# Twelve projection slots by chunk, the bias table by matmuls beside the gathers, sinks and GLA products on GpSimd

## The reference

```python
mod = silu(c) @ w_ada + b_ada                  # 6144 numbers: shift1, scale1, gate1, shift2, scale2, gate2
h = rms_norm(x, norm1_g) * (1 + scale1) + shift1
proj = h @ w_in                                # q_g k_g v_g a_lr r_g (gated linear attention), q_s k_s v_s
log_a = log_sigmoid(a_lr @ w_gla_alpha + b_gla_alpha) / 16
o_gla = rms_norm(gla(q_g, k_g, v_g, log_a)) * silu(r_g)      # chunks of 64 tokens, 4 heads
o_swa = rms_norm(softmax attention, 8 heads, window of 128, ALiBi, one sink per head)
x = x + gate1 * (concat(o_gla, o_swa) @ w_out)
x = x + gate2 * peer(modulate(x, norm2_g, shift2, scale2))   # top 16 of 128x128 experts, 8 heads
```

## Time and profile before

| what | value |
|---|---|
| times of three runs | 1479.94 us median, 1479.8 to 1480.45 |
| profiled execution | span 1480.7 us, first to last instruction |
| busy in the span | TensorE 1311.9, VectorE 933.9, ScalarE 655.4, GpSimd 390.6 us |
| granted TensorE clock, mean | 0.979 |
| DMA | 422.51 MB, 285 GB/s in the mean; software queue 303.71 MB |

### The profile page before, as it was taken

One profiled execution on the slowest core, in us unless ns is written; L12 is line 12 of the kernel. 1 busy time (PEld: TensorE's weight loads), 2 busy tenths in 40 slices (PEclk: granted clock), 3 DMA queues, 4 the chain that ended last, 5 costly groups with the idle time before them and its releaser, 6 DMA issues.

```text
span 1480.7 us, 21207 instructions
## 1 busy us (share of the span) xinstructions
PE 1311.9 (89%) x6932; PEld 936.0 (63%) x6932; DVE 933.9 (63%) x2248; ACT 655.4 (44%) x1801; POOL 390.6 (26%) x432
## 2 busy tenths in 40 slices
PE   6999979888988777878777887999999998999998
PEld 3889934444443222333222476999998987899897
DVE  6678586766667667667754555655556635655555
ACT  3434434344343333333333335545455248544554
POOL 4111144444544444444444142200001005100000
PEclk9999999999999999999999998999999999999999
DMA  8875599999999999999999621665556630445554
GB/s 332 333 254 200 182 422 420 421 421 421 421 421 422 421 422 421 422 421 422 421 422 421 268 89 37 234 219 182 182 182 238 196 102 14 157 149 188 187 185 144
DMA packets 81341, 422.51 MB, mean 285 GB/s; under 512 B 10144, under 2 KB 11472, under 8 KB 48368
## 3 DMA queue, kind: packets, MB, share of 16 engines
q0 software_dynamic: 46656, 303.71, 50.1%
q1 hardware_dynamic: 33280, 114.68, 23.3%
q10 hardware_dynamic: 1328, 3.15, 0.6%
HBM read 418.88 MB, written 2.62 MB: 285 GB/s over the span
## 4 chain that ended last, share of the span: by engine, by line
PE 55%; DMA 27%; DVE 8%; ACT 5%; issue 2%; POOL 1%; DVEq 0%; ACTq 0%; SPq 0%; POOLq 0%
DMA big<-in_experts,R 26%; PE pacc L1136 8%; PE pu L663 6%; PE pu L664 6%; PE pu L665 6%; PE pu L632 3%; DVE big L2380 3%; PE pu L644 2%; PE pacc L663 2%; PE pacc L664 2%; PE pacc L665 2%; PE pacc L720 2%; PE pacc L722 2%; PE pacc L721 2%; ACT L1455 1%
## 5 line engine op out<-in xcount | busy, mean ns | idle before, releaser
L1136 PE MATMUL pacc<-big,early_l 128*128 128x512 f32 x1024 | 492.7, 622 | 119.5 <-ACT early_l L1455 119.2
L1136 PEld LDWEIGHTS pacc<-big,early_l 128*128 128x128 f32 x1024 | 188.1, 195 | 408.4 <-issue 406.1
L2380 DVE CUSTOM_DVE_ANT_0 big<-big,early_h 128x1024 f32<-128x1024 f32 x256 | 311.8, 1224 | 204.9 <-DMA big<-in_experts,R 203.8
L535 POOL DMA_INDIRECT big<-in_experts,R x256 | 288.1, 1125 | 378.7 <-PE pacc L1136 334.3
L436 DVE TENSOR_TENSOR ring_lo<-ring,ring_hi 128x512 fp32r<-128x512 f32 x328 | 214.7, 696 | 195.0 <-ACT ring_hi L429 194.9
L429 ACT ACTIVATE ring_hi<-ring 128x512 fp32r<-128x512 f32 x328 | 187.6, 620 | 123.5 <-PE pu L665 49.4
L1455 ACT ACTIVATE R<-R 128x1 f32<-128x1 f32 x256 | 51.6, 202 | 322.3 <-DVE R L2380 322.1
L663 PE MATMUL pu<-X2h,ring_hi 128*128 128x256 f32 x512 | 146.2, 286 | 3.2 <-DVE big L2497 3.2
L665 PE MATMUL pu<-X2h,ring_lo 128*128 128x256 f32 x512 | 145.6, 284 | 0.0
L664 PE MATMUL pu<-X2l,ring_hi 128*128 128x256 f32 x512 | 145.4, 284 | 0.0
L663 PEld LDWEIGHTS pu<-X2h,ring_hi 128*128 128x128 f32 x512 | 98.9, 193 | 4.2 <-DVE big L2497 3.6
(11 more groups left out here) (408 smaller groups left out, 2097.4 us busy)
## 6 DMA issues: line engine op xcount, KB each, us to landing
ring<-in_weights SPq DMA_DIRECT2D x216, 512.0 KB, 3.5
big<-in_ada POOLq DMA_DIRECT2D x40, 512.0 KB, 6.3
big<-in_w POOLq DMA_DIRECT2D x12, 512.0 KB, 7.1
big<-in_experts,R POOLq DMA_INDIRECT x256, 20.0
bias_row<-big ACTq DMA_DIRECT2D x1, 1536.0 KB, 19.8
XT<-in_xT ACTq DMA_DIRECT2D x1, 1024.0 KB, 8.2
scr<-in_ada POOLq DMA_DIRECT2D x2, 512.0 KB, 12.3
tk<-in_ada POOLq DMA_DIRECT2D x2, 512.0 KB, 14.0
```

Of the source, the lines that this page charges most:

```text
L535: pool.indirect_dma_start(out=pair_rows[:, m % PAIR_SLOTS, :], out_offset=None, in_=experts_d, in_offset=bass.IndirectOffsetOnAxis(ap=expe ...
L1136: last = mm(paccf[:, tt * D + half * 512:tt * D + (half + 1) * 512], diagonal[:, m % 16, :], pair_rows[:, m % PAIR_SLOTS, D + half * 512:D ...
L2380: v.tensor_tensor_reduce(out=pair_rows[:, m % PAIR_SLOTS, 0:D], in0=pair_rows[:, m % PAIR_SLOTS, 0:D], in1=h2_rows[:, u % TT, :], scale=1. ...
```

## The change

Twelve of the 18 slots of w_in (q_s, k_s, q_g, half of k_g, v_s and three quarters of v_g) are loaded by rows instead of by columns: one array of [8, 128, 1536], 768 KB for each chunk, into four buffers, issued by SyncE when the second half of x has landed. TensorE multiplies chunk c as soon as ScalarE has made it: eight tiles into the eight places of `pacc`, the tokens' four into the two banks of `pu`. Six slots stay in the ring. The first 16 modulation rows come as eight pairs of 1 MB through four buffers. 24 bf16 matmuls on zeros stand at the start.

```diff
+FIRST_TILES, FIRST_TOKENS = 8, 4
+SWA_AFTER = (range(0, 2), range(0), range(2, 6), range(6, 11), range(11, 20))
+BIAS_AT, BIAS_GROUP = 104, 64
@@ SyncE
+            sp.wait_ge(s["x_late_loaded"], 16)
+            for c in range(FIRST_BUFS):
+                first_load(c)
...
+            for c in range(FIRST_BUFS, C):
+                first_load(c)
             for k in range(RING):
-                if k < 2:
-                    sp.wait_ge(s["ada_used"], 8 + 4 * k)
+                if k < RING - 1:
+                    sp.wait_ge(s["first_used"], C + 1 - FIRST_BUFS + k)
+                else:
+                    sp.wait_ge(s["early_psum"], TT + FIRST_TILES)
@@ TensorE
             pe.wait_ge(s["casts_made"], 1)
+            full_array(24, pu[:, 0, 0:T])
+            for c in range(C):
+                if c % 4 == 0:
+                    pe.wait_ge(s["x_sq"], c // 4 + 1)
...
-            for h in range(NH):
-                if h >= 2:
-                    pe.wait_ge(s["row_copied"], h - 1)
-                mm(row_bank(h)[:, 0:BROW], relb_all[0:NB, h, :], oneh[0:NB, :], start=True, stop=True)\
-                    .then_inc(s["row_psum"], 1)
...
             for c in range(C):
                 pe.wait_ge(s["h_chunks"], c + 1)
+                last = mm(pn[0:16, 0:T], walr[:, c, :], HTf[:, c, :], start=(c == 0), stop=(c == C - 1))
...
+                for tt in range(TT):
+                    last = mm(pu[:, tt, :], HTf[:, c, tt * P:(tt + 1) * P], w[:, FIRST_TILES * P:FIRST], start=(c == 0),
+                              stop=(c == C - 1))
...
+                for j in range(FIRST_TILES):
+                    last = mm(pacc[:, j, :], w[:, j * P:(j + 1) * P], HTf[:, c, :], start=(c == 0 and j % 2 == 0),
+                              stop=(c == C - 1), skip_group_check=True)
+                    if c == C - 1:
+                        last.then_inc(s["early_psum"], 1)
+                        if j == 2:
+                            log_decay()
...
-            for i in range(17):
+            for i in range(5):
+                if i < 2:
+                    pe.wait_ge(s["tok_out"], i + 1)
...
                 if i == 0:
+                    pe.wait_ge(s["consts_made"], 2)
+                    pe.wait_ge(s["la_parts"], 1)
+                    pe.wait_ge(s["tok_out"], TT)
+                    pe.wait_ge(s["early_out"], FIRST_TILES)
+                for step in SWA_AFTER[i]:
+                    if step == 18:
+                        pe.wait_ge(s["gla_ops"], 1)
+                        pe.wait_ge(s["att_biased"], swa_units)
+                        gla_scores(0)
+                    swa_step(step)
+            gla_scores(1).then_inc(s["gla_scores"], 1)
```

A load of a chunk from the fifth on waits until TensorE has used the buffer (`first_used`). On ScalarE the twelve outputs are copied out as two of 128x512 and eight of 128x256: two before the log decay's Identity, Abs, Exp and Ln, six behind them, then the slots 0 and 1 of the ring, then the five exponents, then slot 2 and the softmax units. On GpSimd:

```diff
+            pool.wait_ge(s["ex_done"], 1)
+            pool.wait_ge(s["early_out"], FIRST_TILES)
+            pool.wait_ge(s["evacs"], USE["w_in"] + 1)
+            for u in range(4, SPAN["swa"][1]):
+                sink(u)
+                if u < 4 + 3 + NSUB:
+                    gla_product(u - 4)
+                if u % 2:
+                    row_load(2 * C + 12 + (u - 5) // 2)
```

A sink waits for the exponent of the unit four before it, and VectorE's maximum waits for the sink. VectorE's share loses the sink copies and the products and shifts the modulation:

```diff
-            modulation(2 * C, 6)
+            modulation(2 * C, 8)
...
-                if i < 12:
-                    modulation(2 * C + 6 + i, 1)
-                if 8 <= i < 8 + 3 + NSUB:
-                    gla_product(i - 8)
+                if 2 <= i < 14 and i % 2 == 0:
+                    modulation(2 * C + 8 + (i - 2) // 2, 1)
...
-            modulation(2 * C + 18, 4)
+            modulation(2 * C + 14, 4)
...
-            modulation(2 * C + 22, 2)
+            modulation(2 * C + 18, 2)
...
-            late_modulation(MOD_EARLY)
-            late_modulation(MOD_EARLY + 1)
+            modulation(2 * C + 20, 2)
...
             split_low(dve, v, "w_out", 2)
+            modulation(2 * C + 22, 1)
             out_residual(1)
             split_low(dve, v, "w_out", 3)
+            modulation(2 * C + 23, 1)
```

Three late rows then stand behind the residuals 5, 6 and 7 of the first token tile, the fourth behind the last residual. The bias table is built beside the gathers 104 to 231, two tokens each, from the one-hot rows (64 partitions: the table's rounded part and its remainder):

```diff
+                for t in bias_tokens(m):
...
+                    last = mm(pu[:, group % 2, t % BIAS_GROUP * NH:(t % BIAS_GROUP + 1) * NH], oneh_r[0:2 * NB, T - 1 - t:T - 1 - t + P],
+                              relb_r[0:2 * NB, :], start=True, stop=True)
```

369 lines of the change are left out of this document (198 added, 171 removed).

## The result

Median 1503.77 us after, 1479.96 before; the ratio is 1.0162, with a 95% interval of 1.0147 to 1.0176. That is slower, as forecast, but by 23.8 us in place of 8.5, and 6.8 above the upper end of the range. One of the changed kernel's four runs took 1555.71 us at a mean granted clock of 0.83 in place of 0.97; it counts in no ratio, and the median without it is 1503.66. The spans of the two profiled executions differ by 21.0 us (1501.7 against 1480.7). The other 2.8 are no cost of the change's steps: in the runs that have both, the time lies 1.6 us above the span for the kernel before and 2.0 for the changed one, so the profiled execution of before took some 1482.3, at the slow end of its own spread (1477.0 to 1482.5 in the rounds of the experiments), where the text had taken its span as a time.

What follows compares the result with a forecast made beforehand. The chain of waits up to the first gather, then DMA at 422 GB/s, bounds the kernel. Bare chain 3.8, clock 3, products 1 and late modulation 1 add 8.8 us to the 1480.7 span: 1488.5, range 1476 to 1497.

Steps and rivals of the forecast that it cites:

- The chunk stage's start: After the sums of squares, root, spread, scaling and shift: chunk work starts at 15.2 to 18.4 us, taken as 16.8.
- Time per chunk: Projections by chunk: TensorE bounds each chunk at 5.7 us, eight chunks 45.8 us; DMA needs 4.2 us for 1.75 MB.
- the warm-up: Start of the chunk stage at the low clock: costs at most 3.3 us, taken as 2.
- What is late next: Log decay through softmax to reciprocal: the chain loses its cover, reciprocal at 125.4 in place of 121.59, +3.8 us.
- The clock: Softmax stretch: TensorE's clock falls in waits, 0 to 8 or 9 us; +3 taken, since dense slots can win it back.
- The GLA products: Seven products moved from VectorE to GpSimd: holding VectorE up costs 0 to 4 us, +1 taken.
- Late modulation and rows: Modulation moved into the output projection, four late rows requested some 20 us later: 0 to 3 us, +1 taken.
- Bias table: Bias matmuls leave the start, 256 small ones go beside the gathers: 0 taken, 45 us at the upper end.
- Rival 4: In the gathers: the bias matmuls overfill TensorE, 1490 to 1530 us; chance 0.03.
- Rival 1: Softmax stretch at its worst: clock low throughout and products block VectorE, 16.8 us slower, 1496.5; chance 0.20.
- Rivals 2 and 3: 2: softmax intervals under 3.4 us, 1474 to 1477, chance 0.22. 3: clock, port, late rows free, 1480 to 1483, chance 0.13.

Runs made afterwards that it cites:

- e3_order: Changed kernel with the first projection chunk requested before x is in, one-hot rows after the chunks, modulation pairs 1 to 3 after x: 1.0125, 1500.0 us.
- e6_fillers: Changed kernel with 32, 20, 16 and 16 matmuls of zeros in TensorE's waits of the softmax stretch: 1.0111, 1496.6 us.
- e1_products_back: Changed kernel with the seven GLA products back on VectorE, sink copies still on GpSimd: 1.0155, 1504.2 us.
- e5_bias_only: Kernel before with only the change's bias table, built by one-hot slices beside the gathers in place of bias matmuls at the start: 1.0008, 1481.7 us.
- e10_hybrid: Changed kernel with eight slots in the chunk stage, first loads reordered, zeros ahead of the sums' second half and units 4, 10 and 14: 1.0060.
- e11_start_and_fillers: Changed kernel, twelve slots early, with first loads reordered, 20 zeros ahead of the sums' second half and zeros in the softmax stretch: 1.0097, 1494.3 us.
- e13_hybrid_ahead: Changed kernel with eight slots in the chunk stage, first loads reordered, narrow products and log decay moved forward, one softmax pair behind each later slot: 1.0006.
- e12_ahead: Changed kernel with narrow products ahead of the tiles, log decay in chunk 3, third chunk buffer in the area of the squares: 1.0105, 1497.1 us.

## Why the prediction was wrong in size

Its sum was 8.8 us on the span; 21.0 were measured. The direction was right; two terms were mis-sized, the start of the chunk stage and the clock. By its own steps:

- **The chunk stage's start, mis-sized: +6.4.** It was put at 16.8 plus a narrow product. Of the difference, 3.4 is the first narrow product at 20.19 in place of 16.8 (x in at 12.36 and the second sums at the low clock, 3.58), 0.6 the narrow product at half speed, 2.5 the wait for the chunk's own load. That load, issued behind x, appeared in the sum nowhere: the text counted 1.75 MB per chunk against TensorE's time per chunk, and did not count what 4 MB of modulation rows, x and c do to the first one. e3_order recovers 2.8 at the log decay. (Three more chunk loads went out right behind the first, on its own queue; how much of the 11.27 us is theirs no run separates.)
- **Time per chunk, 5.90 for 5.7: +1.4** over seven chunks; the warm-up, 2, was right (chunk 0 took 7.46, 2.1 more than the 5.36 of a warm one without its narrow product).
- **What is late next: the mechanism right, the total partly by luck.** With the clock up, log decay to reciprocal takes 63.4 for 63.0, but its parts were off by 3.4, -1.0 and -2.0 and cancel. The pairs pace it, at 5.1 us each (e6), where the text took 4.5 in the mean: exponents to GLA scores 33.7 for 30.3; but log decay to exponents 17.9 for 18.9, and GLA scores to reciprocal 11.8 for 13.8.
- **The clock, taken at the wrong end: +5.** 8.0 by e6_fillers, 3 taken. The argument that slots 3 and 4 are dense and win the clock back was half right: slot 3 ran its first 2.9 us at 0.50 (4.92 in all) and did win it back, but the next wait took it again.
- **The GLA products: -1** (e1_products_back: 72.0 without the move, 71.4 with it).
- **Late modulation and rows: right at the end, by luck.** Up to the first gather's request they cost 2.1 where 1 was taken, and the gather then landed 1.7 faster than before, which the text did not foresee; from the reciprocal to the end 0.9 are left (20.1 to 21.0).
- **Bias table: right,** and e5_bias_only adds that taking its matmuls away at the start was worth nothing either. Rival 4 is out.

6.4 + 1.4 + 5 - 1 is 11.8 of the 12.2 missing. Rival 1 (all of clock and port) had the clock right, at 1496.5; with the start as it was it would have given 1504, but partly by luck: its port and late rows, 3 and 2, measured about 0 and 1, and the 2.8 us between spans and times make up for them. Rivals 2 and 3 are out: from the scores of a pair to those of the next the changed kernel took at least 5.0 us, and the clock was not free. The range was too narrow: the bounds of its terms add up to 12.9 us above the forecast, 1501, and not to the 1496 that the text gives, and the 1.6 for the start held no term for a load that is queued behind others; 6.4 were measured.

## What to carry to other kernels

When work is moved to the front of a kernel, list the bytes that must land before its first instruction and the queue order in which they were asked for, and only then its rate per piece. Work that hid a chain is worth what it hid: before accumulating twelve slots early, ask what then stands beside the softmax, and keep enough of it back (eight slots early, e10_hybrid, were 5.5 us better by the ratios than twelve, e11_start_and_fillers, and with the log decay moved forward, e13_hybrid_ahead, their time equals that of the kernel before). Where slots of 3.65 us stood behind waits of 3 to 5 us and small bursts, each began at the low clock and lost 0.9 to 1.3 us; price that for every piece and not once. Matmuls on zeros in the waits avoided it where they started before the clock fell; look behind the last of them too, where it fell once more in e11_start_and_fillers.

## What the runs showed of the hardware

- A VectorE operation with one input tile, the scaling of 128x128 fp32, was held up by GpSimd products whose lengths are 1.25 to 1.28 us: 2.04, 1.77 and 1.31 us in place of 0.29, and 4.16 us where three products followed each other, though GpSimd had issued a DMA and made a copy of 0.20 us between the last two. Beside a modulation on VectorE (1.21) a product took 2.25.
- 32 bf16 matmuls of zeros of 256 columns take 3.67 us at the high clock and 4.71 where it had fallen first; 84 of them spread over 30 us held TensorE at 1.00 throughout and returned 8.0 us in e6_fillers; in e11_start_and_fillers the clock fell to 0.50 some 8 us behind the last of them.
- A load of 768 KB, requested 8 to 11 us behind 4 MB of modulation rows on another queue, took 11.27 us from request to landing; one of the same size requested 5 us later, behind three of its kind (e12_ahead), took 23.41; the second half of x landed at 12.36 where x whole was in at 10.8.
- A matmul of 8 columns with its load of 64x128 fp32r weights took 0.27 us in the median beside the gathers, two behind each other 0.38, and DMA stayed at 419 to 423 GB/s.
